# Seven half-block products for twelve of the 22 steps of the up projections

## The reference, cut to what matters

```python
def conv_ffn(h, w_up, conv_w, conv_b, w_down):      # h: (S, 1024), w_up: (1024, 5632)
    S = h.shape[1]
    u = h @ w_up
    up = jnp.pad(u, ((0, 0), (CONV_W - 1, 0), (0, 0)))
    u = conv_b + sum(conv_w[j] * up[:, j:j + S] for j in range(CONV_W))   # three taps over tokens
    gate, val = jnp.split(u, 2, axis=-1)
    return (jax.nn.silu(gate) * val) @ w_down       # w_down: (2816, 1024)
...
x = x + conv_ffn(rms_norm(x, norm_ffn[layer]), f_w_up[layer], ...)
```

## Time and profile before

| | us |
|---|---|
| median of 3 runs (lowest, highest) | 1191.81 (1190.55, 1193.16) |
| profiled execution | 1191.57 |
| its span | 1189.8 |
| PE busy | 1174.8 |
| DVE busy | 862.7 |
| ACT busy | 617.0 |
| POOL busy | 348.5 |

### The profile page before, as it was taken

One profiled execution on the slowest core, in us unless ns is written; L12 is line 12 of the kernel. 1 busy time (PEld: TensorE's weight loads), 2 busy tenths in 40 slices (PEclk: granted clock), 3 DMA queues, 4 the chain that ended last, 5 costly groups with the idle time before them and its releaser, 6 DMA issues.

```text
span 1189.8 us, 18961 instructions
## 1 busy us (share of the span) xinstructions
PE 1174.8 (99%) x6874; PEld 999.6 (84%) x6874; DVE 862.7 (73%) x1502; ACT 617.0 (52%) x1033; POOL 348.5 (29%) x429
## 2 busy tenths in 40 slices
PE   9999999999999999999999999999999999999998
PEld 7768886778888888888999887988888888888998
DVE  6588968945766566579897898855766666579986
ACT  6554337855434333345565789945534334335563
POOL 0633547830042522211000366730042421211000
PEclk9999999999999999999999999999999999999999
DMA  7555352253398785436554110053387574326553
GB/s 281 182 187 199 142 202 65 73 142 106 106 238 238 199 217 184 175 109 211 186 160 138 62 37 2 1 125 107 106 192 179 156 172 130 106 71 208 176 173 127
DMA packets 51555, 174.54 MB, mean 147 GB/s; under 512 B 4720, under 2 KB 6128, under 8 KB 41504
## 3 DMA queue, kind: packets, MB, share of 16 engines
q1 hardware_dynamic: 36352, 127.51, 31.3%
q0 software_dynamic: 15136, 46.14, 16.3%
HBM read 171.50 MB, written 52.47 MB: 188 GB/s over the span
## 4 chain that ended last, share of the span: by engine, by line
PE 93%; DVE 3%; ACT 2%; issue 1%; POOL 0%; DVEq 0%; ACTq 0%; POOLq 0%
PE ps L2554 28%; PE ps L2556 27%; PE ps L2555 27%; PE ps L2269 3%; PE ps L2253 3%; PE ps L2069 1%; PE ps L2520 1%; PE ps L2110 1%; PE ps L2237 1%; PE ps L2140 1%; ACT probs L977 1%; DVE w_lo L1705 1%; DVE xT L1725 0%; PE ps L2121 0%; ACT w_hi L1148 0%
## 5 line engine op out<-in xcount | busy, mean ns | idle before, releaser
L2554 PE MATMUL ps<-h_hi,w_hi 128*128 128x512 f32 x704 | 274.4, 390 | 0.0
L2555 PE MATMUL ps<-h_lo,w_hi 128*128 128x512 f32 x704 | 273.9, 389 | 0.0
L2556 PE MATMUL ps<-h_hi,w_lo 128*128 128x512 f32 x704 | 273.9, 389 | 0.0
L1394 DVE TENSOR_TENSOR w_lo<-raw,w_hi 128x2048 fp32r<-128x2048 f32 (+1 forms) x62 | 123.0, 1984 | 118.3 <-ACT w_hi L887 118.3
L1216 ACT ACTIVATE cv<-u_in,vec 128x512 f32<-128x512 f32 x88 | 71.2, 816 | 180.4 <-DVE u_in L1835 178.3
L887 ACT ACTIVATE w_hi<-raw 128x2048 fp32r<-128x2048 f32 (+1 forms) x72 | 121.8, 1692 | 69.1 <-PE ps L2556 69.1
L2554 PEld LDWEIGHTS ps<-h_hi,w_hi 128*128 128x128 f32 x704 | 132.2, 188 | 27.6 <-issue 0.7
L2556 PEld LDWEIGHTS ps<-h_hi,w_lo 128*128 128x128 f32 x704 | 132.2, 188 | 27.6
L2555 PEld LDWEIGHTS ps<-h_lo,w_hi 128*128 128x128 f32 x704 | 132.2, 188 | 27.3
L762 POOL TENSOR_TENSOR v<-act 128x256 f32<-128x256 f32 x16 | 43.3, 2707 | 345.2 <-DVE act L1872 345.2
L2554 PE MATMUL ps<-a_hi,w_hi 128*128 128x256 f32 (+1 forms) x440 | 138.9, 316 | 2.2 <-DVE a_lo L1709 2.2
(11 more groups left out here) (276 smaller groups left out, 2421.6 us busy)
## 6 DMA issues: line engine op xcount, KB each, us to landing
raw<-in_f_up SPq DMA_DIRECT2D x44, 1024.0 KB, 5.0
w_sums<-in_f_w_down POOLq DMA_DIRECT2D x22, 1024.0 KB, 8.7
w_sums<-in_f_w_down POOLq DMA_DIRECT2D x44, 512.0 KB, 9.0
raw<-w_sums SPq DMA_DIRECT2D x44, 512.0 KB, 4.2
raw<-in_a_in_wide SPq DMA_DIRECT2D x12, 1024.0 KB, 6.1
raw<-in_f_w_down SPq DMA_DIRECT2D x22, 512.0 KB, 3.9
raw<-in_f_w_down SPq DMA_DIRECT2D x22, 256.0 KB, 4.0
bias_tiles<-bias_rows SPq DMA_DIRECT2D x1, 4096.0 KB, 27.0
```

Of the source, the lines that this page charges most:

```text
L1394: dve.tensor_tensor(w_lo[:, s, 0:n], raw[:, s, 0:n], w_hi[:, s, 0:n].bitcast(F32), ALU.subtract)\
L2554: pe.matmul(dst, s_hi, m_hi, start=start, stop=False)
L2555: pe.matmul(dst, s_hi, m_lo, start=False, stop=False)
L2556: return pe.matmul(dst, s_lo, m_hi, start=False, stop=stop)
```

## The change

Steps 5 to 8 of layer 0 and 1 to 8 of layer 1 (`SEVENS`) compute a 2 x 2 arrangement of half blocks with seven products instead of eight (features 0 to 511 and 512 to 1023; tokens 0 to 255 and 256 to 511; gate and value channels). A product is 24 matmuls of 256 columns. Five things come with it:

- Weights of all steps but step 0 come in units of 1024 columns (512 KB) in a ring of four: seven units in a seven step, four in another.
- Four sums or differences of the activations are made once in a layer (`gained_features` on ACT, `sums_of_features` on DVE, then rounded and remainder by `sum_hi` and `sum_lo`).
- Four combinations of weights per seven step are made in DRAM by POOL's DMAs: two copies (`copy_up`, 1 MB each), then three accumulating ones (`two_up` 1 MB, `three_up` and `four_up` 512 KB each), each kind behind a wait for all DMAs of the kind before in that layer (`z == 0`). The copies of layer 0 go out between the `pool_lo`, those of layer 1 in its projections; the accumulating ones among the units of attention.
- Four of the seven products follow each other in one PSUM bank, which ACT copies out (`keep`) between them; DVE adds the parts up (`first_row`, `second_row_sum`, `second_row`).
- The work on a seven step's channels is done during the next step; `copy_weights` and `sum_weights` are moved, and POOL's `gate_sums` from the fourth on waits for the last seven step.

```diff
+SEVENS = ((5, 6, 7, 8), (1, 2, 3, 4, 5, 6, 7, 8))
...
+def sums_made(l, tensors):
+
+    return 16 * (SUMS_AT_UP[l] + tensors * len(SEVENS[l]))
...
+            def two_up(l, z):
+
+                if z == 0:
+                    pool.wait_ge(up_sums, sums_made(l, 2))
+                pool.dma_start(w_two[l][z], f_up[l, SEVENS[l][z], 1], accum_op=ALU.add, max_dma_last_dim=8192)\
+                    .then_inc(up_sums, 16)
+
+            def three_up(l, z):
+
+                if z == 0:
+                    pool.wait_ge(up_sums, sums_made(l, 3))
+                pool.dma_start(w_more[l][z][:, 0:D], w_two[l][z][:, D:2 * D], accum_op=ALU.add).then_inc(up_sums, 16)
...
             for u in range(POOL_LO[0], POOL_LO[1]):
+                j = u - POOL_LO[0]
+                if j < 8:
+                    copy_up(0, j // 2, j % 2)
                 pool_lo(u)
-                copy_weights(0, 1 + u - POOL_LO[0])
+            for z in range(4):
+                two_up(0, z)
...
                 normed(0, u)
                 for ahead in masked_behind(u):
                     mask_bias(ahead)
+                if 5 <= u < 9:
+                    three_up(0, u - 5)
+                if 12 <= u < 16:
+                    four_up(0, u - 12)
...
                 if w in KV_LO_BEHIND:
                     kv_lo(KV_LO_BEHIND.index(w))
+                copy_up(1, w, 0)
...
                     key_tails(w)
+                    copy_up(1, w - 2 * T, 1)
...
                 normed(1, u)
                 if u and next_split(u - 1):
                     keys_lo(*next_split(u - 1))
+                if 1 <= u < 9:
+                    two_up(1, u - 1)
+                elif 10 <= u < 14:
+                    three_up(1, 2 * (u - 10))
+                    three_up(1, 2 * (u - 10) + 1)
+                elif 15 <= u < 19:
+                    four_up(1, 2 * (u - 15))
+                    four_up(1, 2 * (u - 15) + 1)
+                elif u >= 19:
+                    copy_weights(1, u - 19)
...
+                gained_features(n // 2)
+                sum_hi(n // 2, 0)
+                sum_hi(n // 2, 1)
                 root_of_mean(n_next)
...
+                sums_of_features(n // 2)
+                sum_lo(n // 2, 0)
+                sum_lo(n // 2, 1)
                 token_rstd(n_next)
...
+                def seven_step(i):
+
+                    banks, z = seven_banks(l, i), SEVENS[l].index(i)
...
+                    for j, (b, moving) in enumerate(((0, 0), (2, 3), (0, 4), (1, 1), (0, 5), (2, 2), (0, 6))):
+                        m = unit_of(l, i, j)
+                        r = m % 4
+                        pe.wait_ge(w_lo_done, U_UP[l] + 2 + m + 1)
...
+                        for part in range(2):
+                            for k in range(4):
```

More of the change, by code:

```diff
@@ L99 @@
 G_COLS = 36
+SEVENS = ((5, 6, 7, 8), (1, 2, 3, 4, 5, 6, 7, 8))
 U_A = 0
 U_AOUT = U_A + 16
+N_UP = [2 + sum(7 if i in SEVENS[l] else 4 for i in range(1, UP_STEPS)) for l in range(2)]
 U_UP = [U_AOUT + KD, 0]
-U_DOWN = [U_UP[0] + 2 * UP_STEPS, 0]
+U_DOWN = [U_UP[0] + N_UP[0], 0]
 U_B = U_DOWN[0] + FT
@@ L108 @@
 U_UP[1] = U_BOUT + KD
-U_DOWN[1] = U_UP[1] + 2 * UP_STEPS
+U_DOWN[1] = U_UP[1] + N_UP[1]
 U_END = U_DOWN[1] + FT
@@ L320, in hybrid_layers_kernel @@
         sb("pad_level4", [P, T])
+        with ExitStack() as scope:
+            v_r = sb("v_r", [P, T, D], F32R, scope)
         v = sb("v", [P, T, D])
@@ L376, in hybrid_layers_kernel @@
         work = a_tmp[:, 0:1152]
+        with ExitStack() as scope:
+            rbc_minus = sb("rbc_minus", [P, S], F32, scope)
         mask = sb("mask", [P, ROW], BF16)
@@ L1208, in feed_forward, with tap2, silu @@
                 n = 2 * l + 1
-                def tap2(i, q, first):
+                def tap2(i, q):
                     ch = l * CT + (q // 2) * FT + 2 * i + q % 2
-                    sc.wait_ge(f_in, 2 * FT * l + 4 * i + q + 1)
-                    if not first:
+                    sc.wait_ge(f_in, IN_AT[l][i] + ((4, 4, 6, 6)[q] if i in SEVENS[l] else q + 1))
+                    if i:
                         sc.wait_ge(f_act, FT * l + 2 * i)
[L1216 to L1233, removed]
+                    sc.activation(cv[:, q, :], u_in[:, q, 2:2 + S], ACT.Identity, bias=conv[:, 3, ch:ch + 1],
+                                  scale=conv[:, 2, ch:ch + 1]).then_inc(f_t2, 1)
+                def silu(i):
                     for q in range(2):
@@ L1242, in step @@
                     else:
[L1243 to L1248, removed]
+                        unit_hi(l, m + 6)
+                        unit_hi(l, m + 7)
+                def seven_step(i):
+                    m, behind = unit_of(l, i), i - 1 in SEVENS[l]
+                    if behind:
+                        tap2(i - 1, 2)
+                        tap2(i - 1, 3)
+                    keep(i, 0)
+                    unit_hi(l, m + 4)
+                    if behind:
+                        silu(i - 1)
+                    keep(i, 1)
+                    unit_hi(l, m + 5)
+                    keep(i, 2)
+                    unit_hi(l, m + 6)
+                    unit_hi(l, m + 7)
+                    keep(i, 4)
+                    unit_hi(l, m + 8)
+                    unit_hi(l, m + 9)
+                    tap2(i, 0)
+                    tap2(i, 1)
+                    unit_hi(l, m + 10)
+                for i in range(UP_STEPS):
+                    if i in SEVENS[l]:
+                        seven_step(i)
+                    else:
+                        plain_step(i)
             first_attention()
@@ L2426, in feed_forward @@
                             ins.then_inc(f_done, 1)
-                channels(0, 2, True, sums=True)
-                channels(0, 3, True, roots=True)
-                with pe.Fori(1, UP_STEPS) as i:
-                    for q in range(4):
-                        channels(i, q, False)
+                channels(0, 2)
+                channels(0, 3)
+                for i in range(1, UP_STEPS):
+                    if i in SEVENS[l]:
+                        seven_step(i)
+                    else:
+                        for q in range(4):
+                            channels(i, q)
             attention(0)
```

374 lines of the change are left out of this document (305 added, 69 removed).

## The result

| | before | after |
|---|---|---|
| median (lowest, highest), 4 runs each | 1191.41 (1190.55, 1193.16) | 1263.62 (1261.08, 1267.35) |
| span of the profiled execution | 1189.8 | 1263.7 |
| PE busy | 1174.8 | 1175.7 |
| PE idle in the span (worked out) | 15.0 | 88.0 |

The change makes the kernel slower: the ratio is 1.0607, interval 1.0573 to 1.064. I had forecast 1223 with a range of 1184 to 1234: slower is right, the size is short by 41 us.

The account below looks back on a forecast made before the run. PE, busy 99% of the span, was taken to bound the kernel. Terms -19.3 + 1 + 3.8 + 0.7 + 8.1 + 2 + 1 + 27 + 5 + 2 = +31.3 on 1191.57 gave 1223 us, range 1184 to 1234.

Parts of the forecast that it names:

- products saved: Seven steps: 20.16 us instead of 21.77, 1.61 less in each of twelve, -19.3 us.
- waits in the seven steps (loads): Unit loads, issued three products ahead, share the DMA engines with `sum_weights`: +1 us (0 to 5).
- starts of the up stages: PE waits at the up stages' start and into step 5: +3.8 and +0.7 us in layer 0, +8.1 in layer 1.
- issues, layer-1 projections: Eight `copy_up` issues of 0.54 us on busy POOL in layer 1's projections: +2 us (0 to 4).
- attention 0: Eight more POOL issues, +1 us (0 to 4), and bias tiles landing late beside accumulations, +5 us.
- attention 1: POOL waits there for accumulating DMAs at 193 GB/s and PE waits behind it: +27 us, 0 kept for the range.
- clock: PE's lower clock around the long waits together: +2 us (0 to 6).
- Rival 3: DVE bounds the seven steps, so they do not get shorter; total above 1240 us, chance 0.05.
- the first scaling: Layer 0's up stage: step 1 wants its result at 319.65 against PE's arrival at 317.5, +2.2 us.
- rivals 1 and 2: Long-row accumulations at the copy's rate, 1189 or 1185 us, chance 0.27; or between both rates, 1193 to 1210, chance 0.10.
- late bias tiles: Start of attention 0: tiles 9.5 us late delay unit 0's probabilities, costing PE 6.8 if rows alternate; +5 taken.
- done at about 724: Attention 1: layer 1's 16 copies, 42 us of DMA work from 678 to 718, finish then; `two_up` waits nearly nothing.

Follow-up runs that it names:

- Early copies: The whole change, but layer 1's sixteen `copy_up` issued behind layer 0's up stage, beside down stage 0: 1272.0 us, ratio 1.0666.
- Layer 0 later: The whole change, but layer 0's accumulations issued behind POOL's units 1 to 4, 12 to 15 and 20 to 23 of attention 0: 1264.01 us, ratio 1.0596.
- No sums: The changed kernel without the transfers that make sums of up weights and their waits; seven steps load plain blocks: 1202.72 us, ratio 1.0093.
- Free sums: The changed kernel with every transfer issued in place, but into memory of its own and without waits; seven steps read plain weights: 1242.19 us, ratio 1.0411.
- Spread: No sums, with layer 1's six `copy_weights` two per step in steps 1 to 3 and its down-weight accumulations from step 4: 1201.52 us, ratio 1.0074.
- Copies in attention 1: Four and four, with layer 1's 19 copies one behind each unit of attention 1 and features' sums spread over steps 0 to 3: 1187.79 us, ratio 0.9961.
- Layer 0 behind: The whole change, but layer 0's twelve accumulations issued behind attention 0, before `copy_weights`: 1257.89 us, ratio 1.0548.
- Four and four: Changed kernel with four seven steps per layer, copies moved ahead, accumulations in up steps 0 to 3, features' sums after step 0: 1222.5 us, ratio 1.0261.

## Why the prediction was wrong in size, point by point

| term | predicted | measured after | from |
|---|---|---|---|
| products saved | -19.3 | -20.6 at 20.05 a step | four intervals between seven steps of layer 1: 80.2 us |
| waits in the seven steps (loads) | +1 | +11.9 | ACT `kept` and `u_in`, 2.5 in layer 0, 9.4 in layer 1 |
| starts of the up stages | +12.6 | +11.9 | 1.3, 2.1, 0.5; 1.5, 0.5, 6.0 |
| issues, layer-1 projections | +2 | +4.3 | 55.2 to 59.5; 55.2 again in *Early copies* |
| attention 0 | +1 and +5 | +10.9 idle | 6.8 at the start |
| attention 1 | +27 | +32.4 idle | POOL's pauses 6.94, 14.35, 8.10 |
| clock | +2 | at most +20.6 of 21.5 | PE busy above its work, with 20.6 saved |

The measured column adds up to 72.3 with 21.5, of the 73.9.

**The steps that held.** Seven steps keep their pace: 20.05 us each, against 20.16 worked out, with DVE busy for 75.18 of 80 and PE never waiting from 1020 to 1100. Rival 3 is out. The waits at the starts came within 0.1 us each: `rstd` 1.3 and 1.5 (1.4), the first scaling 2.1 (2.2), `rbc_minus` 0.5 (0.6), `w_lo` 6.0 (6.1). The accumulations cost what their bytes cost, with rows of 8 KB as with those of 2 KB in the earlier trace rows: the first `three_up` came 43.2 us after the first `two_up`, against 43.5 worked out from the earlier trace rows. The windows of the first `two_up`s and of POOL's last pause behind them:

```profile
753.00:780.00 27.00, 25.41 (x228) 21.20 (x229) 18.80 (x58) 19.54 (x55) 24.62 (x37) 0.89 0.99 201
780.00:795.00 15.00, 3.03 (x24) 2.71 (x23) 4.30 (x18) 4.70 (x15) 1.53 (x2) 0.71 0.96 199
```

201 and 199 GB/s: rivals 1 and 2 are out. The estimate that the Trainium skill ("DMA: Bandwidth & Descriptors", Anatomy of one DMA) gives, 19 + 2 us for eight of them, does not hold here for accumulating DMAs with 8 KB rows either; they took 43.2. At the start of attention 0 late bias tiles were to cost 6.8 and PE waited 6.8 there, a wait that is gone in *Layer 0 later*. The equal figure is luck: it was to come by POOL's probabilities and the turning behind them, with the tiles 9.5 late; they were 11.7 late, and PE waited for `neg_max`, for which DVE itself needed a bias tile.

**The steps that failed.** The waits had the right causes; terms of the sum were sized too small, three above all.

1. *Clock, +2.* The largest miss. PE's 20.2 us of extra busy time (with 19.3 saved) are 9.5 in attention 1, 4.1 in and ahead of attention 0, 3.0 in the up stage of layer 1, and the rest beside them. I had priced little more than one short stretch (3.4 us at the lower level, which cost 1.7). But each long wait brings one: PE spent some 68 us of the span at the lower level, 41 of them in attention 1, in three stretches that each begin during a pause of POOL and last beyond it:

   ```profile
   748.80:759.00 10.20, 4.56 (x12) 2.78 (x12) 1.39 (x3) 1.22 (x4) 6.33 (x10) 0.50 0.70 163
   786.35:803.40 17.05, 4.96 (x20) 3.95 (x22) 1.71 (x4) 2.94 (x6) 7.52 (x13) 0.50 0.83 157
   820.50:834.10 13.60, 8.71 (x36) 7.17 (x38) 4.85 (x13) 4.49 (x13) 11.86 (x18) 0.50 0.80 127
   ```

   PE is busy for 18.2 us in them and for 41.2 in all stretches at the lower level. At twice the clock the same work takes at least half of that, so an estimate from these rows is that the clock costs at most 9.1 of the 9.5 in attention 1, and at most 20.6 in all. In *No sums*, attention 1 has the clock at 1.00 and is busy for 63.7 us, as before. Not all of it need be clock: in *Free sums* attention 1 has a clock of 0.98 and PE is still busy for 67.95 us, 4.3 more than before, of which by the same estimate at most 1.7 are clock (3.4 us at the lower level). That matmuls overlap less between short waits would explain the rest; it is not shown.
2. *Seven-step loads, +1.* I had counted bytes and not where they stand: six copies of 1 MB issued at once behind step 0 of layer 1, just when units are first needed every 2.88 us. The landings of the units went to 10.4 us there (11.2 in *No sums*), beyond the three products ahead. *Spread* shows that those copies caused the waits, and *Copies in attention 1*, where none stands in the up stage, that its 218.0 us can be had with accumulations beside the seven steps.
3. *Attention 1, +27, "done at about 724".* The copies were done at 752.67, which is about 730.5 in the times of the kernel before (attention 1 begins 22.2 later). I had let them run at the 401 GB/s of the earlier trace rows, and misread that row: from 479 to 482 a load moved 0.66 MB beside 0.54 MB of the copy. From 481 to 483 the copy was alone, at 393 GB/s. In a row the copies of layer 1 moved less; the first of these rows has 1.05 MB of loads in its 7.08, the second nothing but copies:

```profile
700.00:722.00 22.00, 17.21 (x108) 14.82 (x107) 16.75 (x38) 15.03 (x33) 19.63 (x32) 1.00 0.95 322
722.00:740.00 18.00, 17.91 (x110) 14.68 (x109) 15.31 (x37) 14.60 (x33) 11.88 (x28) 1.00 0.99 335
```

So a pause of 6.94 stands in front that I did not have, and the one behind the `two_up`s is 14.35 instead of 18. *Early copies* takes the first away, and attention 1 is 6.3 us shorter.

The term for POOL's issues in layer 1's projections, +2, counted eight copies at 0.54; sixteen stand there, the first eight of them at 0.65 to 0.73, and it came to 4.3.

Attention 0 (+6, measured 16.0 in all) failed by the same kind of step: the first tiles were priced right, the later ones at nothing. *Layer 0 later* shows that a later tile waits as well.

Why nothing moved for free: *Free sums*, *Layer 0 behind*, *Early copies* and *Four and four* each put transfers beside another stage, and each time that stage gave back 7 to 28 us. Plain copies beside attention 1, which moves only 9 GB/s by itself, are the exception.

## What to carry to other kernels

Price a transfer that accumulates by its bytes at the accumulating rate (here some 200 GB/s, against 335 to 393 for copies), and look where the instruction that waits for it stands: a wait in the queue of an engine that others follow costs its full length, and again in the clock behind it. When units become smaller, the time by which loads run ahead shrinks with them; look at the landing times under load and not at the bytes per step. A saving of 7% in a stage is soon gone: here it paid only with fewer seven steps, their preparation in stages that load little, and the sums of features split over steps.

## What I had not expected of the hardware

- DRAM-to-DRAM copies issued one after the other by POOL moved 335 GB/s with nothing beside them (722 to 740), a single one 393 (kernel before, 481 to 483).
- Accumulations of 8 KB rows moved 199 to 201 GB/s, the 2 KB rows 193. Cutting the rows to 2 KB made eight of them 2.8 us longer (46.0 against 43.2) and attention 1 10.1 us longer, but let 2 KB tiles of another queue land 5.4 us earlier.
- Copies beside the down stage 0 cost it 21 us (16 copies) and 28 us (19 copies), at 282 and 290 GB/s; 19 copies beside attention 1, at 294 GB/s, cost 2.1 us. The total rate does not tell what a neighbour suffers. The stages differ in their own traffic, 174 GB/s in the down stage (*Copies in attention 1*) and 9 in attention 1 before, which would explain it.
